# A two-layer hybrid decoder step: head outputs transposed half a pair of tiles later, Sigmoids ahead of two weight halves, one conditioning block moved in the ring

## The reference

```python
def mixer_branches(u, pos, lw, st, mla_past):
    z = u @ lw['w_in'] + lw['b_in']
    (a_q, a_k, a_v, a_o, a_i, a_f, b_q, b_kv, b_kr, c_glu,
     d_q, d_k, d_v, d_g, gates) = jnp.split(z, IN_OFFSETS, axis=-1)
    h_a, C1, n1, m1 = mlstm(...)                       # mixer a, 4 heads
    y_a = jax.nn.sigmoid(a_o) * layer_norm(h_a).reshape(B, T, -1)
    o_lat = mla_sample_attention(q_abs, q_pe, ckv, kpe, mla_past)   # mixer b, paged cache
    y_c, buf1 = conv_module(c_glu, buf0, ...)          # mixer c: 31 taps, layer norm, silu
    o_d, S1 = retention(qd, kd, heads(d_v, D_HEADS), S0)            # mixer d, 4 heads
    y_d = jax.nn.silu(d_g) * layer_norm(o_d).reshape(B, T, -1)
    ys = jnp.stack([y_a, y_b, y_c, y_d], axis=2)
    proj = jnp.einsum('btnw,nwd->btnd', ys, lw['w_branch'])
    g = jax.nn.sigmoid(gates.reshape(B, T, N_BRANCH, D_MODEL))
    out = jnp.sum(g * proj, axis=2) @ lw['w_out']

def trunk_layer(x, c, pos, lw, st, mla_past):
    mod = jax.nn.silu(c) @ lw['w_ada'] + lw['b_ada']   # the conditioning
    sh1, sc1, g1, sh2, sc2, g2 = jnp.split(mod[:, None, :], 6, axis=-1)
    mix, new_st = mixer_branches(x * (1.0 + sc1) + sh1, pos, lw, st, mla_past)
    x = layer_norm(DEEPNORM_ALPHA * x + g1 * mix, lw['ln1_g'], lw['ln1_b'])
    f = (jax.nn.silu(u2 @ lw['w1']) * (u2 @ lw['w3'])) @ lw['w2']   # u2 = x * (1 + sc2) + sh2
```

## Time and profile before

| | |
|---|---|
| median of three runs | 1726.92 us (1726.02 to 1727.75) |
| the profiled execution | 1724.7 us, span 1722.5 |
| TensorE busy | 1641.3 us (95%) |
| VectorE, ACT, POOL busy | 854.9, 738.1, 727.8 us |
| mean granted clock of TensorE | 0.989 |
| HBM read, written | 291.81 MB, 13.94 MB |

### The profile page before, as it was taken

How to read it: one execution, slowest core, us unless ns; L and a number is a source line. 1 busy time by engine, 2 the same in 40 slices (tenths; PEclk the granted TensorE clock), 3 DMA queues, 4 the chain that set the end, 5 groups by cost and what they waited for, 6 DMA issues and landing times. The chain is left out here.

```text
span 1722.5 us, 29957 instructions
## 1 busy us (share of the span) xinstructions
PE 1641.3 (95%) x11040; PEld 1422.9 (83%) x11040; DVE 854.9 (50%) x1961; ACT 738.1 (43%) x1135; POOL 727.8 (42%) x465
## 2 busy tenths in 40 slices
PE   6999999999999999999979999999999999999996
PEld 3887889877668889999967878898866688899996
DVE  2464378666431575332255534876854325833323
ACT  3455634323534364443354554442244333644423
POOL 2444557646123443333343435665552135433332
PEclk9999999999999999999989999999999999999998
DMA  9465335328674544446634653362476845344440
GB/s 370 152 225 196 110 118 194 130 100 293 218 283 160 221 177 147 150 147 212 216 129 172 207 185 94 121 221 95 148 286 221 286 153 220 143 157 157 152 147 31
DMA packets 73522, 307.67 MB, mean 179 GB/s; under 512 B 15842, under 2 KB 25506, under 8 KB 43426
## 3 DMA queue, kind: packets, MB, share of 16 engines
q1 hardware_dynamic: 73378, 305.77, 50.2%
HBM read 291.81 MB, written 13.94 MB: 178 GB/s over the span
## 5 line engine op out<-in xcount | busy, mean ns | idle before, releaser
L2528 POOL TENSOR_TENSOR wlx<-ring,wh 128x1024 fp32r<-128x1024 f32 x171 | 409.3, 2394 | 570.2 <-ACT wh L1311 562.0
L502 PE MATMUL zps<-uhi,wh 128*128 128x320 f32 x1232 | 379.5, 321 | 3.0 <-DVE qabs L1884 1.7
L503 PE MATMUL zps<-ulo,wh 128*128 128x320 f32 x1232 | 366.5, 310 | 0.0
L1311 ACT ACTIVATE wh<-ring 128x1024 fp32r<-128x1024 f32 x172 | 182.3, 1060 | 354.4 <-PE zps L503 206.2
L2658 POOL TENSOR_TENSOR wlo<-ring,whi 128x1024 fp32r<-128x1024 f32 x66 | 162.3, 2460 | 288.4 <-ACT whi L1274 287.8
L502 PEld LDWEIGHTS zps<-uhi,wh 128*128 128x128 f32 x1232 | 233.6, 190 | 15.7 <-issue 8.4
L503 PEld LDWEIGHTS zps<-ulo,wh 128*128 128x128 f32 x1232 | 233.7, 190 | 0.9
L507 PE MATMUL zps<-uhi,wlx 128*128 128x320 f32 x1232 | 206.6, 310 | 0.0
L507 PEld LDWEIGHTS zps<-uhi,wlx 128*128 128x128 f32 x1232 | 187.6, 189 | 0.0
L1274 ACT ACTIVATE whi<-ring 128x1024 fp32r<-128x1024 f32 x132 | 140.1, 1061 | 99.5 <-PE zps L1011 91.9
L1009 PE MATMUL zps<-xhi,whi 128*128 128x320 f32 x560 | 173.5, 310 | 2.1 <-ACT gt L1274 1.8
(11 more groups left out here) (394 smaller groups left out, 2665.3 us busy)
## 6 DMA issues: line engine op xcount, KB each, us to landing
ring<-wpack_dram SPq DMA_DIRECT2D x218, 1024.0 KB, 5.0
arena<-cache_dram SPq DMA_DIRECT2D x128, 320.0 KB, 4.8
arena<-stateA_dram SPq DMA_DIRECT2D x2, 2064.0 KB, 9.6
o_cn_s<-arena SPq DMA_DIRECT2D x2, 2064.0 KB, 7.7
arena<-stateD_dram SPq DMA_DIRECT2D x2, 2048.0 KB, 12.7
o_ret_s<-arena SPq DMA_DIRECT2D x2, 2048.0 KB, 9.6
arena<-wpack_dram SPq DMA_DIRECT2D x4, 1024.0 KB, 8.9
x<-x_dram SPq DMA_DIRECT2D x2, 1280.0 KB, 10.0
```

Of the source, the lines that this page charges most:

```text
L502: nc.tensor.matmul(o, hi[:, k * P:(k + 1) * P], xh[:, k, :], start=k == 0, stop=False)
L503: last = nc.tensor.matmul(o, hi[:, k * P:(k + 1) * P], xl[:, k, :], start=False, stop=False)
L1311: nc.scalar.activation(wh[:, i, :], ring[:, g % RING, i * 1024:(i + 1) * 1024], ACT.Copy).then_inc(*ev("act_hq", (q, i), layer=layer))
L2528: G().tensor_tensor(low_ring(SPLIT[q])[:, half], ring_of(SPLIT[q])[:, half], wh[:, i, :], ALU.subtract).then_inc(*ev("pool_l", (q, i)))
```

## The change

Five edits in one. The list SLOTS has ada 16 in slot 2 ahead of branch(2, 0), where it stood in slot 3 behind gate(2, 4). The blocks then come as g2_0, g2_2, ada 16, branch(2, 0), g2_4, where they were g2_0, g2_2, branch(2, 0), g2_4, ada 16; the start of slot 3 moves with it. In mixer a TensorE transposes the heads' outputs after tiles dg0, dg1 and dg2, which was after dv3, dg0 and dg1. In mixer d it turns token tile 2, with the state pair behind it, after g3_3, which was after g3_2 (the pair after g3_3 as before). ACT has the last two Sigmoids of branch three ahead of the two high halves of g2_0, and between them one small Exp that brings in the table. VectorE weighs head 3 of mixer a one rotation sooner, and spreads the taps differently about head_gate.

```diff
--- before.py
+++ after.py
@@ -71,7 +71,7 @@
 
 
 
-SLOTS = [[("gate", 2, 0)], [("gate", 2, 2)], [("branch", 2, 0)], [("gate", 2, 4), ("ada", 16)], [("gate", 2, 6), ("ada", 17)],
+SLOTS = [[("gate", 2, 0)], [("gate", 2, 2)], [("ada", 16), ("branch", 2, 0)], [("gate", 2, 4)], [("gate", 2, 6), ("ada", 17)],
          [("branch", 2, 4), ("ada", 18)], [("gate", 1, 0), ("ada", 19)], [("gate", 1, 2)], [("gate", 1, 4)]]
 CONV_NORM = 1
 SLOT_START = []
@@ -786,7 +786,7 @@
                         in_tiles((f"{x_}{j}", f"{x_}{j + 1}"), [("dve_dk", (x_, h)) for h in (j, j + 1)], fill=fill)
 
                     def plain_tile(x_, j, *fill):
-                        in_tiles((f"{x_}{j}", f"{x_}{j + 1}"), [("act_d", (x_, h)) for h in (j, j + 1)], fill=fill)
+                        in_tiles((f"{x_}{j}", f"{x_}{j + 1}"), [("act_d", (x_, h)) for h in (j, j + 1)], fill=fill or (None, None))
 
                     def pair_a(p):
                         return lambda: state_pair("a", p, W)
@@ -796,9 +796,9 @@
                     turned_tile("dq", 0, None, pair_a(1))
                     turned_tile("dq", 2, None, pair_a(2))
                     plain_tile("dv", 0, None, pair_a(3))
-                    plain_tile("dv", 2, None, lambda: turn_heads("a", 0))
-                    plain_tile("dg", 0, lambda: turn_heads("a", 1), lambda: turn_heads("a", 2))
-                    plain_tile("dg", 2, None, None)
+                    plain_tile("dv", 2)
+                    plain_tile("dg", 0, lambda: turn_heads("a", 0), lambda: turn_heads("a", 1))
+                    plain_tile("dg", 2, lambda: turn_heads("a", 2), None)
 
 
                     def channel_sum(name, src, k, ready, freed_by):
@@ -903,6 +903,10 @@
                         for t in ts:
                             turn_heads("d", t)
 
+                    def last_turn():
+                        turn_heads("d", 2)
+                        state_pair("d", 2, P)
+
                     def last_pair(i):
                         if i == 1:
                             state_pair("d", 3, P)
@@ -914,7 +918,7 @@
                     gate(0, 6, None, lambda: outputs("d", 1, P))
                     branch(0, 4, first_states)
                     gate(3, 0, None, lambda: turns_d(0))
-                    gate(3, 2, lambda: turns_d(1, 2), lambda: state_pair("d", 2, P))
+                    gate(3, 2, lambda: turns_d(1), last_turn)
                     branch(3, 0, last_pair)
                     gate(3, 4)
                     gate(3, 6)
@@ -1541,7 +1545,11 @@
                     pair_keys("d", 3)
                     gates(3, 1, 1)
                     gates(3, 2, 2)
-                    gates(3, 4)
+                    gates(3, 4, 2)
+                    gates(3, 6, 2, follow=False)
+                    go("act_s", "early", stats[:, 31:32], ones[:, 0:1], ACT.Exp)
+                    after("g3_6", 0)
+                    after("g3_7", 1)
 
                     def conv_squares():
                         act.wait_ge(*times("out_conv", 32))
@@ -2156,8 +2164,8 @@
                                 nc.vector.scalar_tensor_tensor(out=o, in0=src, scalar=wk, in1=part_sum, op0=ALU.mult, op1=ALU.add).then_inc(*ev("dve_c", ("tap", j, k)))
 
                     rotate("dk", 0)
+                    weigh("a", 3)
                     rotate("dk", 1)
-                    weigh("a", 3)
                     rotate("dk", 2)
                     head_rows("a", 1, W)
                     rotate("dk", 3)
@@ -2169,8 +2177,9 @@
                     head_norm("a")
                     state_update("a", W, 3)
                     spread_queries("d")
-                    head_gate("a", 0, 0, 1, 2)
-                    taps(22)
+                    for t, count in enumerate((6, 6, 10)):
+                        head_gate("a", 0, t)
+                        taps(count)
 
                     def gated(n, half, *tiles, behind=0):
                         for i in tiles or range(4):
@@ -2208,12 +2217,14 @@
                     gated(0, 4, 3)
                     state_update("d", P, 1)
                     head_norm("d")
-                    head_gate("d", 3, 0, 1, 2)
+                    head_gate("d", 3, 0, 1)
+                    taps(5)
+                    head_gate("d", 3, 2)
                     state_update("d", P, 2)
                     gated(3, 0, 0, 1, behind=4)
                     state_update("d", P, 3)
                     gated(3, 0, 2, 3, behind=4)
-                    taps(24)
+                    taps(19)
                     gated(3, 4, behind=4)
 
                     def conv_center():
```

## The result

The changed kernel is slower: 1740.39 us median over eight executions (1735.98 to 1746.69), against 1727.34 (1726.02 to 1732.22). The forecast was slower, at 1732.7, with 1737.0 as the end of the range; the sign was right and the size a factor of two short. Both kernels spread by 6 to 11 us from one execution to the next. So sizes of effects are taken from ratios over several executions here, and the traces, one execution each, say where.

What follows compares the result with a forecast made beforehand. TensorE, busy 1641.3 of 1722.5 us, was taken to bound the kernel. Gains -5.92, stalls +9.19 and clock +2.5 gave +5.8, so a median of 1732.7; own range 1729.5 to 1736, 8-in-10 range 1726.5 to 1737.

Steps and rivals of the forecast that it cites:

- SLOTS: Ahead of branch(2,0): g2_4's late load makes ACT hold up the Silus; waiting costs 4.40 and 4.79 us, together +9.19.
- The weighing: Mixer a, head 3's weights earlier: wait at L712 goes, the next wait grows by as much; 0, bounds 0 and -2.8.
- the stall: TensorE's wait ahead of branch(2,0) for the Silus: some 6.0 and 6.4 us, where it stood 1.62.
- Mixer d: Waits of 1.37 and 1.94 at L721 go; 0.25 and 0.8 come back at branch(3,0), 1.1 left per layer.
- Mixer a's turns: Mixer a, transposes half a pair later: L721 wait for VectorE's state update goes, -1.1 us per layer; bounds 0 and -1.1.
- Sigmoids and Exp: L434 waits of 1.27 and 1.84 go, cached pages limit next; the first turn's 0.72 goes in each layer.
- The clock behind the stall: At branch(2,0), lower clock costs 2.0 us per layer, in layer one replacing 1.46: +0.5 and +2.0; bounds -1.46 and +3.3.
- The rule that the prediction weighed: Idle gaps between matmul bursts halve the clock; both stalls at full price, +3.3 in place of +2.5, median 1733.5.
- the rivals: Three: weights in time (chance 0.10), a stall without the clock (0.15), the gains don't come (0.09).
- the gains don't come: Rival, chance 0.09: mixer and slot 0 gains fail, +11.0; with half of mixer a's and d's gains +8.9, 1735.8.

Runs made afterwards that it cites:

- the filled stall: The changed kernel with ada 16's sixteen matmuls issued six times, where TensorE stood idle: 1734.03 us, ratio 1.0029 to the kernel before.

## Why the prediction was right in sign and short in size

- *SLOTS.* Right in place, cause and, within the interval, size: forecast 4.40+4.79 of waiting and +2.5 of clock, 11.7; alone it measured 9.0 (5.7 to 12.3). Waits 6.07 and 6.11 for 6.0 and 6.4. Moving ACT's halves behind the Silus took all of it away with the load still late.
- *The weighing: the step that failed first.* The prediction had "VectorE's total is the same, so that wait grows by what the first one gave. I take 0; bounds 0 and -2.8". The wait grew so (2.29 for 1.25+0.78). But two short waits became one, and the lower clock came behind it in every trace; +4.0 us (0.7 to 7.4) alone, 2.3 by the starts. The bound above was missing; the clock had been priced for the stall only.
- *Mixer d: the second.* The sum for VectorE was right: 3.91 us from the first to the third head_gate were forecast (1.49+2.0+0.42), and alone it took 4.01. But the prediction looked for the next wait at branch(3,0), which reads y, and took 0.25 and 0.8. It came earlier, at the state pair, since this takes the bank that the turn had just filled: 1.07 and 1.64, again with a lower clock behind, in both layers of the changed kernel. Forecast -2.2; alone +0.3 (-2.6 to +3.3), and -4.7 without the five taps.
- *Mixer a's turns.* Right: -2.2 forecast, -2.6 measured.
- *Sigmoids and Exp.* The place was right: the cached pages are next, 1.39 and 1.04, where under 1 was forecast. Of -5.92 in all, mixer d's -2.2 and mixer a's -2.2 leave -1.5 for this; it measured -1.0 (-3.1 to +1.0), which says little of the size.
- *The clock behind the stall.* Forecast +0.5 and +2.0; in the trace the sixteen matmuls took 6.01 for 6.00 and 6.09 for 4.54, so 0 and +1.55. The rule that the prediction weighed (the Trainium skill, "TensorE: Matmul & The Clock Gate", "Why this matters for your kernels") agrees with the trace in that the clock did fall at both stalls, 0.55 in layer one and 0.50 in both layers of SLOTS alone. Its price would have brought the forecast 0.8 nearer to the time, for the wrong place: what was missed stood behind short waits.
- *The sum of the misses.* By the ratios, 11.9-5.8 = 6.1. The weighing has 4.0 of it, mixer d 2.5, the Sigmoids 0.5; SLOTS gives back 2.7 and mixer a's turns 0.4. That leaves 2.2, less than the interval of any one of them. By the table it is 11.1-5.8 = 5.3: mixer a has 2.7 of it, mixer d with the Sigmoids 3.7, and the stall gives back 1.1.

None of the rivals was it. The one nearest in time, "the gains don't come", had about the right sum (+11.0 with none of them, 1735.8 with half) for a reason that is wrong in the main: the gains of mixer a's turns came, and were eaten by the wait and the lower clock that the weighing made, and mixer d's by those at the state pair.

## What to carry to other kernels

A ring makes every block wait for the one three places before it: when a block is moved forward, look at what is pushed back, which engine waits for that landing, and what stands behind the wait in that engine's own order. When small work is moved to directly ahead of other small work, look whether it takes the same bank. And when two short waits of TensorE are merged into one, price the clock behind it, not only the idle time.

## What the runs showed of the hardware

The granted clock fell behind waits far shorter than the stall, and not by their length alone. A wait of 2.3 to 2.5 us beside the 32-row products of the states (L745): a fall ten times of ten. One of 1.05 to 1.64 at mixer d's state pair, with as small matmuls: eight times of ten. One of 1.4 to 1.9 at L721, between full tiles: twice in twelve. The others of a like length had none behind them: 1.1 at L721 in twelve, 1.2 to 1.6 at L712 in eighteen, 1.0 to 1.9 for the gate's Sigmoid at L434 in fourteen, 1.0 to 1.5 for the cached pages in eight. One of 1.62 ahead of branch(2,0), behind the narrow products of the cached attention: nine times in fourteen; with 0.45 or none there, never in eight, and with 1.65 and 1.80 behind the 96 matmuls of the filled stall, never in two. Each fall of these short waits costs 1.5 to 1.7 us, but for one that lasted twice as long and cost 3.1. What TensorE did ahead of these waits differs, and which part of it decides was not tried. That the same wait falls on either side from one execution to the next would account for much of the spread of 6 to 11 us; this was read from one trace of each kernel and not shown.
